# Experts stage: the second product's weight transfers move from SyncE's queue to ScalarE's

## The chip, the cores and the metric

The kernel runs on one core of a Trainium2 chip. The metric is device time in microseconds (us), the median of the timed runs. Engines are named as the profile names them: PE is TensorE, DVE VectorE, ACT ScalarE, POOL GpSimd, SP SyncE. SP computes nothing; its queue issues DMA transfers. ACT and POOL have queues that issue transfers too, between their computing instructions, and every engine works its own queue strictly in order.

## The reference, cut to what matters

Two transformer blocks follow each other. The change touches only the last large piece, the mixture of experts of the second block: every token goes to 2 of 32 experts, and each expert is a gated product.

```python
xs = xf[tok]
hid = jax.nn.silu(lax.ragged_dot(xs, w1, group_sizes)) * lax.ragged_dot(xs, w3, group_sizes)
ys = lax.ragged_dot(hid.astype(xs.dtype), w2, group_sizes) * gate.reshape(-1)[order][:, None].astype(xs.dtype)
```

Here there are 1024 tokens, the model is 1024 wide and an expert 512 wide. w1 and w3 are the weights of the first product ("up"), w2 those of the second ("down").

## The kernel before, in words

The tokens, sorted by expert, are laid out in blocks of 128 slots that each belong to one expert. How many blocks there are is known only at run time (`last_pair`); in the profiled execution it is 36, since 288 up tiles of weights were loaded and a block takes 8. A block b needs 12 weight tiles of 128x1024 float32, 512 KB each: 8 up tiles, which land in `raw_up[:, n]`, and 4 down tiles, which land in `raw_down[:, k]`. Each of these twelve places exists once, so a tile's successor can be asked for only when both halves of the split below have read it.

Float32 products are made of two reduced halves. ACT copies a raw tile into `w_high` (the "raise": `raise_up` L2668, `raise_down` L2678). A second engine subtracts it from the raw tile into `w_low` (the "lower"): DVE for up tiles (`lower_up` L2728), POOL for down tiles (`lower_down` L2591). PE then multiplies high by high, high by low and low by high: `step` L2646 to L2648 for up tiles, `multiply_down` L2631 for down tiles. The split tiles stand in a ring of 6 slots.

The engines run one software pipeline, skewed by a block: step b raises, lowers and multiplies the up tiles of block b, and does the down part of block b-1. Steps 0 and 1 are written out, steps 2 to 35 run in a loop of two steps per turn (`over_pairs`), and a tail finishes block 35. The order is written out by hand in each engine's `step`:

- ACT: raise up 0 and 1; `x_high` L2698; raise up 2 to 5; `hid_high` L2683; raise up 6 and 7; `store` L2688, a DMA that writes the output of block b-2 after waiting for `y_out` from DVE; raise down 0; `silu` L2712; raise down 1 to 3.
- DVE: lower up 0; `hidden` L2734; lower up 1; `x_low` L2759; lower up 2 to 5; `lower_hidden` L2738; `copy_out` L2748; lower up 6 and 7.
- POOL: `gather` (L2580 to L2584, an indirect DMA for block b+2), then lower down 0 to 3.
- PE: up tiles 0 to 7; transposes of the next x; `multiply_down(b-1)`; transposes of the hidden block.
- SP: `load`, 8 up tiles of block b, each after the lower of its predecessor (semaphore `up_low`), and then `load_down(b-1)`, 4 down tiles, each after POOL's lower of its predecessor (semaphore `down_low`).

The expert's number is read from the table `m.owner` into a register by `value_load`, once in `load` and once in `load_down`. The wait that the change carries from one queue to the other is this, k = 0 to 3:

```python
earlier(sp, down_low, 4 * (b - 1) + k + 1)
sp.dma_start(raw_down[:, k], d["w2"][ds(expert, 1), :, k].rearrange("a p n -> p (a n)")
```

With b standing for the block whose tiles are loaded, it says that POOL has lowered tile k of the block before it.

Of the kernel before, what the change touches and what calls it, by code (L numbers as in the profile page):

```python
# [27 lines left out]
ds = bass.ds  # L28
# [26 lines left out]
EXPERTS = GROUPS * PER_GROUP  # L55
# [8 lines left out]
HT = DE // P  # L64
# [566 lines left out]
def two_banks(ps, bank):  # L631
    return ps[:, bank:bank + 2, :].rearrange("p b (k n) -> p (b k) n", n=P)
# [1838 lines left out]
def stage_experts(nc, d, m):  # L2471
# [4 lines left out]
    with ExitStack() as ctx:  # L2476
# [3 lines left out]
        def sem(name):  # L2480
            return nc.alloc_semaphore(name)

        def two(name):
# [4 lines left out]
        raw_up, raw_down = m.raw_up, m.raw_down  # L2488
# [15 lines left out]
        up_loaded, down_loaded = m.up_loaded, m.down_loaded  # L2504
        indexed, gathered, stored = (two("moe_" + n) for n in ("indexed", "gathered", "stored"))
        up_high, up_low, up_used, down_high, down_low, down_used = (sem("moe_" + n) for n in (
            "up_high", "up_low", "up_used", "down_high", "down_low", "down_used"))
# [6 lines left out]
        def up_slot(n):  # L2514
            return n % RING

        def down_slot(k):
            return (UPS + k) % RING

        def over_pairs(eng, body):  # L2520


            last = eng.value_load(m.last_pair[0:1, 0:1], min_val=SLOTS_MIN // (2 * P) - 1,
                                  max_val=BLOCKS // 2 - 1)
            for s in range(2):
                body(0, s, s)
            with eng.Fori(1, last + 1) as i:
                for s in range(2):
                    body(i, s, 2)
            return last  # L2530

        def earlier(eng, sem, value):

            if not isinstance(value, int) or value > 0:
                eng.wait_ge(sem, value)

        def up_slot_free(eng, b, n):

            if n < 2:
                earlier(eng, up_used, 8 * b - 1 + n)  # L2540
            elif n < RING:
                earlier(eng, down_used, 4 * (b - 2) + n - 1)
            else:
                eng.wait_ge(up_used, 8 * b + n - 5)

        @block.sync
        def _(sp):
            def load_down(b):
                if isinstance(b, int) and b == 0:
                    return  # L2550
                expert = sp.value_load(m.owner[0:1, ds(b, 1)], min_val=0, max_val=EXPERTS - 1)
                for k in range(HT):

                    earlier(sp, down_low, 4 * (b - 1) + k + 1)
                    sp.dma_start(raw_down[:, k], d["w2"][ds(expert, 1), :, k].rearrange("a p n -> p (a n)")
                                 ).then_inc(down_loaded[k], 16)

            def load(i, s, before):
                b = 2 * i + s
                if isinstance(b, int) and b == 0:  # L2560
                    return
                expert = sp.value_load(m.owner[0:1, ds(b, 1)], min_val=0, max_val=EXPERTS - 1)
                for n in range(UPS):
                    j, k = n // HT, 2 * (n % HT)

                    earlier(sp, up_low, 8 * (b - 1) + n + 1)
                    sp.dma_start(raw_up[:, n].rearrange("p (k n) -> p k n", k=2),
                                 d["w13"][ds(expert, 1), :, j, k:k + 2].rearrange("a p k n -> p (a k) n")
                                 ).then_inc(up_loaded[n], 16)
                if before:  # L2570
                    load_down(b - 1)

            last = over_pairs(sp, load)
            load_down(2 * last + 1)

        @block.gpsimd
        def _(pool):
# [85 lines left out]
        @block.scalar  # L2663
        def _(act):
            def raise_up(b, n):
                act.wait_ge(up_loaded[n], 16 * (b + 1))
                up_slot_free(act, b, n)
                act.activation(w_high[:, up_slot(n)], raw_up[:, n], ACT.Copy).then_inc(up_high, 1)  # L2668

            def raise_down(b, k, end=False):  # L2670
                act.wait_ge(down_loaded[k], 16 * (b + 1))
                if end:

                    act.wait_ge(down_used, 4 * (b - 1) + k + 1)
                else:

                    act.wait_ge(up_used, 8 * (b + 1) + k + 3)
                act.activation(w_high[:, down_slot(k)], raw_down[:, k], ACT.Copy).then_inc(down_high, 1)  # L2678

            def turned_hidden(b):  # L2680
                act.wait_ge(hid_turned, b + 1)
                earlier(act, down_used, 4 * b)
                act.activation(hid_high[:].rearrange("p k n -> p (k n)"), ps[:, 4, :], ACT.Copy  # L2683
                               ).then_inc(hid_high_out, 1)

            def store(b, o):
                act.wait_ge(y_out, NH * b + NH)
                act.dma_start(d["y_rows"][ds(b * P, P), :], y[o]).then_inc(stored[o], 16)  # L2688

            def step(i, s, before):  # L2690
                b = 2 * i + s
                ahead = 2 if before else RING
                for n in range(ahead):
                    raise_up(b, n)
                act.wait_ge(x_turned, b + 1)

                earlier(act, up_used, 8 * b)
                act.activation(x_high[:], two_banks(ps, 0), ACT.Copy).then_inc(x_high_out, 1)  # L2698
                for n in range(ahead, RING):
                    raise_up(b, n)  # L2700
                if before:
                    turned_hidden(b - 1)
                for n in range(RING, UPS):
                    raise_up(b, n)
                if before > 1:
                    store(b - 2, s)
                if before:
                    raise_down(b - 1, 0)
                act.wait_ge(up_used, 8 * b + 4)

                earlier(act, hid_turned, b - 1)
                act.activation(hid[s], ps[:, 2, :], ACT.Silu).then_inc(silued, 1)  # L2712
                if before:
                    for k in range(1, HT):
                        raise_down(b - 1, k)

            last = over_pairs(act, step)
            turned_hidden(2 * last + 1)
            for k in range(HT):
                raise_down(2 * last + 1, k, end=True)  # L2720
            store(2 * last, 0)
            store(2 * last + 1, 1)

        @block.vector
# [405 lines left out]
```

## Time and profile before

| | us |
|---|---|
| timed runs, median (3 runs) | 3482.81 |
| timed runs, lowest and highest | 3479.39, 3483.36 |
| profiled execution, own time | 3477.42 |
| profiled execution, span of its core | 3475.6 |
| experts stage in it, steps 2 to 35 | some 2726 to 3400 from the span's start |

The trace gives for each engine its instructions with start and duration, the idle time before one and what ended it. Times are from the span's start. A row of the timeline merges instructions of one line that follow each other without a pause (x3, x4); "idle before" stands in brackets. The DMA share is the mean busy share of the core's 16 DMA engines, and PEclk is the granted clock of TensorE, 1.00 for 2.4 GHz and 0.50 for 1.2 GHz. Where an instruction waits for several semaphores, the view names the one that came last.

### The profile page before, as it was taken

The numbers are of one execution on the slowest core, as the hardware profiler recorded it, in microseconds if no ns is written. First come the engines' busy times: TensorE is split into PE (matmuls) and PEld (weight loads), VectorE is DVE, ScalarE is ACT, GpSimd is POOL, SyncE is SP. The second block draws the span as 40 slices with busy tenths as digits, with TensorE's granted clock in tenths as the row PEclk, the third lists the DMA queues.
The fourth block names the chain that finished last, engine by engine and source line by source line (L and its number), as shares of the span: only waits on it lengthen the run. The fifth ranks groups of instructions, "written<-read, shape, count | busy, mean of one in ns | idle before, by whom it ended". The sixth has DMA issues, their size and how long they took to land. (4 is left out here: it accounts for less than half of the span.)

```text
span 3475.6 us, 40486 instructions
## 1 busy us (share of the span) xinstructions
PE 3099.1 (89%) x14608; PEld 2226.9 (64%) x14608; DVE 1532.0 (44%) x2000; ACT 1130.9 (33%) x1517; POOL 1123.1 (32%) x567
## 2 busy tenths in 40 slices
PE   8999999989999999859898997999594899999993
PEld 5666666468888788624444445999342777777772
DVE  4444444421111211346300444444425778778775
ACT  3333332011111122211210221222201677777773
POOL 1101110223333344410001113222000588787784
PEclk9999999999999999979899998999796999999996
DMA  2000002111111132155200014000303899999995
GB/s 92 25 19 19 31 19 81 77 49 48 48 48 48 65 129 95 63 201 181 99 25 29 25 43 164 13 13 1 134 1 133 320 370 372 366 371 371 368 374 212
DMA packets 116290, 446.94 MB, mean 129 GB/s; under 512 B 14658, under 2 KB 15618, under 8 KB 111314
## 3 DMA queue, kind: packets, MB, share of 16 engines
q1 hardware_dynamic: 102740, 393.66, 30.7%
q0 software_dynamic: 7984, 28.66, 2.5%
q10 hardware_dynamic: 5456, 23.10, 1.6%
q8 instruction: 75, 1.23, 0.1%
q14 instruction: 35, 0.29, 0.0%
HBM read 401.18 MB, written 44.10 MB: 128 GB/s over the span
## 5 line engine op out<-in xcount | busy, mean ns | idle before, releaser
L2728 DVE TENSOR_TENSOR moe_w_low<-moe_raw_up,moe_w_high 128x1024 fp32r<-128x1024 f32 x288 | 438.3, 1560 | 153.7 <-ACT moe_w_high L2668 153.7
L2591 POOL TENSOR_TENSOR moe_w_low<-moe_raw_down,moe_w_high 128x1024 fp32r<-128x1024 f32 x144 | 419.6, 2944 | 143.2 <-ACT moe_w_high L2678 143.2
L2668 ACT ACTIVATE moe_w_high<-moe_raw_up 128x1024 fp32r<-128x1024 f32 x288 | 304.7, 1061 | 188.8 <-PE ps L2631 111.6
L91 PE MATMUL ps<-x1T_high,w_up_high 128*128 128x512 f32 x704 | 274.7, 390 | 3.5 <-PEq L2949 3.5
L91 PE MATMUL ps<-x1T_low,w_up_high 128*128 128x512 f32 x704 | 274.4, 390 | 0.0
L91 PE MATMUL ps<-x1T_high,w_up_low 128*128 128x512 f32 x704 | 274.3, 390 | 0.0
L2646 PE MATMUL ps<-moe_w_high,moe_x_high 128*128 128x512 f32 x576 | 228.7, 397 | 4.0 <-DVE moe_x_low L2759 4.0
L2648 PE MATMUL ps<-moe_w_high,moe_x_low 128*128 128x512 f32 x576 | 225.7, 392 | 0.0
L2647 PE MATMUL ps<-moe_w_low,moe_x_high 128*128 128x512 f32 x576 | 225.3, 391 | 0.0
L781 POOL TENSOR_TENSOR w_up_high<-w_up,consts 128x1024 fp32r<-128x1024 f32 x44 | 83.6, 1899 | 382.7 <-PE ps L91 285.3
L446 DVE TENSOR_REDUCE top<-ps 128x1 f32<-128x256 f32 (+7 forms) x128 | 91.0, 753 | 240.3 <-PE ps L342 240.2
L279 POOL TENSOR_TENSOR qkv_low<-qkv_raw,qkv_high 128x1024 fp32r<-128x1024 f32 x22 | 53.6, 2436 | 438.0 <-ACT qkv_high L578 438.0
L296 PE MATMUL ps<-x0T_high,qkv_high 128*128 128x512 f32 x384 | 162.9, 424 | 22.8 <-DVE x0T_low L483 10.0
L80 PE MATMUL ps<-xT,w_cols 128*128 128x512 f32 x384 | 170.7, 598 | 0.0
L80 PE MATMUL ps<-w_rows,xT 128*128 128x512 f32 x384 | 165.5, 593 | 0.0
L561 ACT ACTIVATE probs<-ps,top 128x256 f32<-128x256 f32 (+7 forms) x128 | 94.0, 739 | 216.4 <-DVE top L446 216.4
L2678 ACT ACTIVATE moe_w_high<-moe_raw_down 128x1024 fp32r<-128x1024 f32 x144 | 147.3, 1056 | 33.3 <-DVE xT L2748 18.2
L974 POOL TENSOR_TENSOR w_down_low<-w_down,w_down_high 128x1024 fp32r<-128x1024 f32 x44 | 106.1, 2413 | 157.0 <-ACT w_down_high L957 157.0
L2631 PE MATMUL ps<-moe_w_high,moe_hid_high 128*128 128x512 f32 x288 | 101.7, 434 | 61.2 <-POOL moe_w_low L2591 61.1
L91 PEld LDWEIGHTS ps<-x1T_high,w_up_high 128*128 128x128 f32 x704 | 132.5, 188 | 31.5 <-issue 3.9
L298 PE MATMUL ps<-x0T_high,qkv_low 128*128 128x512 f32 x384 | 151.7, 395 | 0.0
L297 PE MATMUL ps<-x0T_low,qkv_high 128*128 128x512 f32 x384 | 151.1, 394 | 0.0
(436 smaller groups left out, 6157.5 us busy)
## 6 DMA issues: line engine op xcount, KB each, us to landing
moe_raw_up<-in_w SPq DMA_DIRECT2D x288, 512.0 KB, 10.4
moe_raw_down<-in_w SPq DMA_DIRECT2D x144, 512.0 KB, 9.7
w_ada<-in_w_ada SPq DMA_DIRECT2D x48, 512.0 KB, 4.9
w_up<-in_ffn_w_up SPq DMA_DIRECT2D x22, 1024.0 KB, 4.8
w_down<-in_ffn_w_down SPq DMA_DIRECT2D x44, 512.0 KB, 3.5
y_rows<-xT ACTq DMA_DIRECT2D x36, 512.0 KB, 8.3
qkv_raw<-in_attn_w SPq DMA_DIRECT2D x22, 512.0 KB, 3.5
y_rows<-zero_rows SPq DMA_DIRECT2D x1, 8192.0 KB, 30.1
```

What stands on the lines that cost most here:

```text
L80: ins = pe.matmul(out, stationary, moving, start=(n == 0), stop=(n == last))
L91: ins = pe.matmul(out, stationary, moving, start=start and n == 0, stop=stop and n == last)
L296: pe.matmul(ps[:, bank, :], w_high[:, s, k, :], x_high[:, k, cols], start=(k == 0), stop=False)
L297: pe.matmul(ps[:, bank, :], w_high[:, s, k, :], x_low[:, k, cols], start=False, stop=False)
L298: return pe.matmul(ps[:, bank, :], w_low[:, s, k, :], x_high[:, k, cols], start=False, stop=(k == DT - 1))
L2591: pool.tensor_tensor(w_low[:, down_slot(k)], raw_down[:, k], w_high[:, down_slot(k)].bitcast(F32), ALU.subtract).then_inc(down_low, 1)
L2646: pe.matmul(ps[:, 2 + j, :], x_high[:, k, :], high, start=first and a == 0, stop=False)
L2647: pe.matmul(ps[:, 2 + j, :], x_high[:, k, :], low, start=False, stop=False)
L2648: ins = pe.matmul(ps[:, 2 + j, :], x_low[:, k, :], high, start=False, stop=last and a == 1)
L2668: act.activation(w_high[:, up_slot(n)], raw_up[:, n], ACT.Copy).then_inc(up_high, 1)
L2678: act.activation(w_high[:, down_slot(k)], raw_down[:, k], ACT.Copy).then_inc(down_high, 1)
L2728: dve.tensor_tensor(w_low[:, up_slot(n)], raw_up[:, n], w_high[:, up_slot(n)].bitcast(F32), ALU.subtract).then_inc(up_low, 1)
```

## The change

`load_down` leaves SP's queue and is written into ACT's, word for word otherwise, its `value_load` and its four waits for `down_low` included. In ACT's `step` it stands right behind `x_high` and ahead of the raises of up 2 to 5; a copy for the last block stands ahead of the tail. SP's queue keeps the up tiles alone. Nothing is added to or taken from what any engine computes, nor from the transfers.

```diff
@@ sync
-            def load_down(b):
-                if isinstance(b, int) and b == 0:
-                    return
-                expert = sp.value_load(m.owner[0:1, ds(b, 1)], min_val=0, max_val=EXPERTS - 1)
-                for k in range(HT):
-
-                    earlier(sp, down_low, 4 * (b - 1) + k + 1)
-                    sp.dma_start(raw_down[:, k], d["w2"][ds(expert, 1), :, k].rearrange("a p n -> p (a n)")
-                                 ).then_inc(down_loaded[k], 16)
-
...
-                if before:
-                    load_down(b - 1)
-
-            last = over_pairs(sp, load)
-            load_down(2 * last + 1)
+
+            over_pairs(sp, load)
@@ scalar
+            def load_down(b):
+                if isinstance(b, int) and b == 0:
+                    return
+                expert = act.value_load(m.owner[0:1, ds(b, 1)], min_val=0, max_val=EXPERTS - 1)
+                for k in range(HT):
+
+                    earlier(act, down_low, 4 * (b - 1) + k + 1)
+                    act.dma_start(raw_down[:, k], d["w2"][ds(expert, 1), :, k].rearrange("a p n -> p (a n)")
+                                  ).then_inc(down_loaded[k], 16)
+
...
                 act.activation(x_high[:], two_banks(ps, 0), ACT.Copy).then_inc(x_high_out, 1)
+                if before:
+                    load_down(b - 1)
                 for n in range(ahead, RING):
                     raise_up(b, n)
...
             last = over_pairs(act, step)
+            load_down(2 * last + 1)
             turned_hidden(2 * last + 1)
```

SP's queue in the loop before, where a step's last up tile (L2567) is followed by the four down tiles (L2555) and these by the next step's read of `owner` (an ISA or REGISTER_ALU row is a wait or register work):

```order
L2567 DMA moe_raw_up<-in_w 128x1024
L2551 ISA
L2551 TENSOR_LOAD owner
L2551 ISA x2
L2535 ISA
L2555 ISA
L2555 DMA moe_raw_down<-in_w 128x1024
...
L2555 DMA moe_raw_down<-in_w 128x1024
L2562 ISA
L2562 TENSOR_LOAD owner
```

The same place in SP's queue of the change, with the lines' new numbers:

```order
L2557 DMA moe_raw_up<-in_w 128x1024
L2552 ISA
L2552 TENSOR_LOAD owner
L2552 ISA x2
L2535 ISA
```

The four down transfers, their waits and one read of `owner` are gone from between two steps' up transfers.

ACT's queue in the loop before, from `x_high` (L2698) over the raises of up 2 to 5 (L2668) to `hid_high` (L2683):

```order
L2698 ACTIVATE moe_x_high<-ps 128x1024
L2535 REGISTER_ALU
L2668 ACTIVATE moe_w_high<-moe_raw_up 128x1024
L2535 REGISTER_ALU
L2668 ACTIVATE moe_w_high<-moe_raw_up 128x1024
L2535 REGISTER_ALU
L2668 ACTIVATE moe_w_high<-moe_raw_up 128x1024
L2535 REGISTER_ALU
L2668 ACTIVATE moe_w_high<-moe_raw_up 128x1024
L2535 REGISTER_ALU
L2683 ACTIVATE moe_hid_high<-ps 128x512
```

The same place in ACT's queue of the change (`x_high` L2695, raises L2655, `hid_high` L2670):

```order
L2695 ACTIVATE moe_x_high<-ps 128x1024
L2676 ISA
L2676 TENSOR_LOAD owner
L2676 ISA x2
L2535 REGISTER_ALU
L2680 ISA
L2680 DMA moe_raw_down<-in_w 128x1024
...
L2680 DMA moe_raw_down<-in_w 128x1024
L2655 ACTIVATE moe_w_high<-moe_raw_up 128x1024 x4
L2670 ACTIVATE moe_hid_high<-ps 128x512
```

The read of `owner`, four waits for `down_low` and four issues now stand between `x_high` and the raise of up 2.

## Rows read from the trace of the kernel before

**Rows 1.** The page: busy time of each engine over the whole span.

```profile
PE 3099.1 (89%) x14608; PEld 2226.9 (64%) x14608; DVE 1532.0 (44%) x2000; ACT 1130.9 (33%) x1517; POOL 1123.1 (32%) x567
```

**Rows 2.** Stretches: length, busy time of PE to POOL, PEclk, DMA share, GB/s.

```profile
2735.00:3395.00 660.00, 605.68 (x2797) 485.30 (x2796) 518.30 (x436) 477.70 (x499) 521.44 (x233) 1.00 0.99 369
2714.00:2735.00 21.00, 17.99 (x80) 14.17 (x81) 19.62 (x14) 16.11 (x18) 14.27 (x6) 1.00 0.86 296
3408.00:3416.00 8.00, 3.85 (x13) 2.89 (x12) 1.89 (x3) 4.38 (x5) 5.75 (x3) 0.79 0.33 126
```

**Rows 3.** Waits in 2735 to 3395: total us, times, longest.

```profile
DVE moe_w_low L2728 <- ACT moe_w_high L2668: 141.7, 33, 4.3
POOL moe_w_low L2591 <- ACT moe_w_high L2678: 128.4, 33, 4.0
```

**Rows 4.** Timeline of POOL, one step: start, us, line, tile.

```profile
2999.55 11.80 POOL L2591 TENSOR_TENSOR moe_w_low<-moe_raw_down,moe_w_high 128x1024 fp32r<-128x1024 f32 x4 [3.85 <-ACT moe_w_high L2678]
3002.28 2.41 POOL L2591 TENSOR_TENSOR moe_w_low<-moe_raw_down,moe_w_high 128x1024 fp32r<-128x1024 f32 x1
3008.00 3.35 POOL L2591 TENSOR_TENSOR moe_w_low<-moe_raw_down,moe_w_high 128x1024 fp32r<-128x1024 f32 x1
3019.49 11.70 POOL L2591 TENSOR_TENSOR moe_w_low<-moe_raw_down,moe_w_high 128x1024 fp32r<-128x1024 f32 x4 [3.93 <-ACT moe_w_high L2678]
```

**Rows 5.** Timeline of DVE in the same step.

```profile
3004.33 1.43 DVE L2728 TENSOR_TENSOR moe_w_low<-moe_raw_up,moe_w_high 128x1024 fp32r<-128x1024 f32 x1 [4.28 <-ACT moe_w_high L2668]
3006.28 2.83 DVE L2728 TENSOR_TENSOR moe_w_low<-moe_raw_up,moe_w_high 128x1024 fp32r<-128x1024 f32 x1
3010.17 2.25 DVE L2728 TENSOR_TENSOR moe_w_low<-moe_raw_up,moe_w_high 128x1024 fp32r<-128x1024 f32 x1
3012.35 1.21 DVE L2728 TENSOR_TENSOR moe_w_low<-moe_raw_up,moe_w_high 128x1024 fp32r<-128x1024 f32 x1
3014.62 1.21 DVE L2728 TENSOR_TENSOR moe_w_low<-moe_raw_up,moe_w_high 128x1024 fp32r<-128x1024 f32 x1
3015.76 0.68 DVE L2738 TENSOR_TENSOR moe_hid_low<-ps,moe_hid_high 128x512 fp32r<-128x512 f32 x1
3016.36 1.27 DVE L2748 TENSOR_TENSOR xT<-ps,mod 128x512 f32<-128x512 f32 x2
```

**Rows 6.** Timeline of ACT in the same step; ACTq is its queue issuing a DMA.

```profile
3003.24 1.06 ACT L2668 ACTIVATE moe_w_high<-moe_raw_up 128x1024 fp32r<-128x1024 f32 x1 [0.30 <-PE ps L2648]
...
3005.62 1.01 ACT L2698 ACTIVATE moe_x_high<-ps 128x1024 fp32r<-128x1024 f32 x1
...
3013.10 1.06 ACT L2668 ACTIVATE moe_w_high<-moe_raw_up 128x1024 fp32r<-128x1024 f32 x1 [2.25 <-PE ps L2631]
...
3017.80 0.34 ACTq L2688 DMA_DIRECT2D y_rows<-xT  x1
3018.34 1.06 ACT L2678 ACTIVATE moe_w_high<-moe_raw_down 128x1024 fp32r<-128x1024 f32 x1 [0.99 <-DVE xT L2748]
...
3019.79 3.01 ACT L2678 ACTIVATE moe_w_high<-moe_raw_down 128x1024 fp32r<-128x1024 f32 x3
...
3028.09 1.06 ACT L2668 ACTIVATE moe_w_high<-moe_raw_up 128x1024 fp32r<-128x1024 f32 x1 [0.31 <-PE ps L2631]
```

**Rows 7.** Timeline of SP's queue: first issue, us to the end of the last, count.

```profile
3002.49 9.35 SPq L2555 DMA_DIRECT2D moe_raw_down<-in_w  x4
3012.77 7.62 SPq L2567 DMA_DIRECT2D moe_raw_up<-in_w  x8
```

**Rows 8.** One line's instructions: SP's transfer issued at 3014.5 (up 3), then `owner` reads (ns).

```profile
DMA to landing us min/median/max: 10.4/10.4/10.4
...
L2551 SPq TENSOR_LOAD <-owner x4: 332/349/447, 3000.7 to 3060.1; - x4
```

**Rows 9.** Timelines behind the loop, block 35: POOL and ACT.

```profile
3399.27 7.10 POOL L2591 TENSOR_TENSOR moe_w_low<-moe_raw_down,moe_w_high 128x1024 fp32r<-128x1024 f32 x3
...
3408.63 0.60 ACT L2683 ACTIVATE moe_hid_high<-ps 128x512 fp32r<-128x512 f32 x1 [8.69 <-PE ps L2656]
```

## The prediction, written before the changed kernel ran

> **What bounds the kernel now.** I began with the page [rows 1]: PE is busy 89% of the span. That is a mean over many stages, and the change touches one, so the stretch of its loop decides. There (the first of [rows 2]) PE is busy 605.68 of 660 us (92%) at a granted clock of 1.00, and the DMA engines show a share of 0.99 at 369 GB/s. Either could pass for the limit. The waits of the stretch [rows 3] speak against both. The two longest are DVE for ACT and POOL for ACT, once in each of 33 steps, and none of the 9 pairs in that view is an engine that waits for a transfer. I therefore followed one step through the timelines and looked for a closed chain without a pause.
>
> A step lasts 19.84 us: POOL's four lowers end at 2999.55 + 11.80 = 3011.35 and one step later at 3019.49 + 11.70 = 3031.19 [rows 4]. The chain between these two ends is:
>
> - POOL's lower of down 3 ends at 3011.35 (the third of [rows 4]).
> - DVE had begun its lower of up 2 at 3010.17, but took 2.25 us over it instead of 1.21 (the third and fourth of [rows 5]); it is held until POOL is through. The next one begins at 3012.35, which is 1.00 us behind POOL's end.
> - DVE runs on without a pause: lowers of up 3 to 5 in steps of (3014.62 - 3012.35) / 2 = 1.135 us, `lower_hidden` at 3015.76, `copy_out` from 3016.36 to 3017.63 [rows 5].
> - ACT waits for this `copy_out` in `store`, issues it at 3017.80 and begins the raise of down 0 at 3018.34 [rows 6].
> - POOL starts 1.15 us later, at 3019.49, and works for 11.70 us [rows 4].
>
> 8.14 us from POOL's end to its start and 11.70 us of POOL's work are 19.84 us. PE is not in this chain, nor is any transfer: up 3 was issued at 3014.5, took 10.4 us [rows 8] and so landed at 3024.9, and ACT raised it at 3028.09 (the last of [rows 6]). The DMA engines are full, yet they deliver 3.1 us early.
>
> The second thing to read is how POOL and DVE treat each other. A lower of POOL lasts 2.41 us by itself (the second of [rows 4]); the one of down 3 took 3.35. DVE's lower of up 1, begun at 3006.28 under POOL's third tile, ends at 3009.11 (the second of [rows 5]); from there to POOL's end at 3011.35 are 2.24 us, one whole lower. The two take turns. Four lowers of POOL would take some 9.4 us by themselves and take 11.80: a step holds it for about 0.4 us at the first tile (3002.28 - 2999.55 is 2.73) and for 1.0 each at the third and the fourth, behind DVE's lowers of up 0 and up 1.
>
> **The change part by part.**
>
> *SP loses four issues, their waits and one read of `owner`.* Today SP is held behind the down tiles: its four issues stretch over 9.35 us, at the pace of POOL's lowers, and the up tiles follow at 3012.77 [rows 7]. Up 0 could be asked for once DVE has lowered its predecessor, at 3004.33 + 1.43 = 3005.76 (the first of [rows 5]), 7 us earlier. Nothing waits for the landing, so this is worth 0. Its cover is the 3.1 us above, and it only grows.
>
> *ACT gains a wait in the middle of its step.* ACT is through with `x_high` at 3005.62 + 1.01 = 3006.63 (the second of [rows 6]). It then reads `owner` (0.35 us by SP's rows for the same read [rows 8]) and issues down 0 and down 1, whose predecessors POOL has lowered at some 3002.3 and 3004.7. Down 2 waits for POOL's third tile (3008.0), and down 3 for the fourth: 3011.35. From 3006.63 to then are 4.7 us, and in them fall the raises of up 2, 3 and 4 today: up 5 begins at 3013.10 behind an idle time of 2.25 us, so these three are done by 3010.85 (the third of [rows 6]). Queued behind the wait are these three, up 5, `hid_high`, up 6 and 7, the store and all raises of the down tiles. DVE waits for the raises, and POOL for the last. The read of `owner` and the first three issues cost nothing, because they lie within these 4.7 us. Only the fourth issue is on the path.
>
> *The price on the chain.* POOL's end is time 0.
>
> - Issue of down 3: SP's fourth ends at 3002.49 + 9.35 = 3011.84 [rows 7], 0.49 behind POOL's end. I take the same 0.49 for ACT: its own issue of the store takes 0.34 us and starts 0.17 behind DVE's end (3017.63 to 3017.80) [rows 5, 6], which is 0.51.
> - From the issue to the next raise: behind the store's issue it is 3018.34 - 3018.14 = 0.20 us [rows 6], with two register instructions between; none stand there in the new order. So between 0.0 and 0.20; I take 0.14, nearer to the only row.
> - Raise of up 2: 1.06 us, and DVE starts 0.03 behind a raise (3003.24 + 1.06 = 3004.30 on ACT, 3004.33 on DVE) [rows 5, 6].
> - DVE's next lower starts one interval of 1.135 us behind.
>
> Together 0.49 + 0.14 + 1.06 + 0.03 + 1.135 = 2.86 us, where it is 1.00 today. A step becomes 1.85 us longer (bounds 1.72 and 1.91). From there on the chain is the same as today, since ACT's raises follow each other in about 1.0 us (three in 3.01 [rows 6]), faster than DVE's lowers. PE spends 605.68 / 660 x 19.84 = 18.2 us on a step's 12 tiles [rows 2], some 1.5 each; behind POOL's end it has one down tile and two up tiles to do before it needs up 2, 4.5 us, and DVE has lowered that by 2.9.
>
> Does POOL's own time stay at 11.70? It shifts as a whole. Up 0 of the next step is raised behind the raises of down 1 to 3, so it too comes some 1.5 to 1.85 us later, and DVE's lowers of up 0 and up 1 again meet POOL's second and third tiles. The lower of up 2 no longer begins under POOL's fourth tile, but by the turns read above it was DVE that was held there, not POOL. Nothing is given back. The Trainium skill's page "SBUF — State Buffer", section "SBUF: two separate sides", has a rule for this: when a DVE instruction with two SBUF inputs meets a GpSimd instruction, the first one keeps the shared port pair for its whole length and the other fully blocks. By that rule the sum stays at 1.85; if the two merely slowed each other, the fourth tile, 0.94 us over its 2.41, would win back about the half of this that falls beside up 2, 0.45, and the sum would be 1.4 (48 us in all). The rows fit the rule.
>
> *Where it counts.* Steps 2 to 35 have the wait: 34 of them. Behind the loop ACT issues block 35's down tiles before `hid_high`; POOL's end there is 3399.27 + 7.10 = 3406.37, and ACT is idle until 3408.63 [rows 9], so this costs 0.
>
> The sum: 34 x 1.85 = 62.9 us on the profiled execution's own 3477.42, which gives 3540.3. The median of the runs shown is 5.4 us (0.15%) above that execution. Against the median the forecast is 3482.8 + 62.9 = 3545.7.
>
> **The rivals.**
>
> *The turns fall otherwise (about 3527).* DVE's lower of up 0 is ready 0.35 us before POOL's second tile ends (3004.33 against 3004.69) [rows 4, 5]. Moved by a little it would fall under the third tile, up 1 would fall behind the fourth, and POOL would be held once less: 1.1 us won, of which some 0.55 is lost again because `x_low` and up 2 come behind the late up 1. A step then costs 1.3 us more: 44 us. For it: the margin is small. Against it: the new order brings up 0 earlier within POOL's work, not later, as the raise no longer waits for PE but only for ACT itself.
>
> *No change (3483).* ACT is idle for 2.25 us before up 5 anyway [rows 6], and 28% of the stretch [rows 2]; one may hope that the wait falls there. Against it: the four lowers of DVE need the raises one by one, and three of them would start only when today they are all done. Or the move is a matter of queues alone: the Trainium skill's page "DMA: Bandwidth & Descriptors", section "Issuing engines are not separate DMA queues", says that transfers of all engines interleave on the same DMA engines and that spreading them saves only issue time. By that rule alone the result would be 0, and what decides here is the wait beside the issue, which it does not speak of.
>
> *Faster: the DMA engines are the limit after all (about 3427).* With SP free, up tiles are asked for up to 7 us earlier, and a share of 0.99 leaves room for the claim. A step could then shrink to PE's own 18.2 us: 34 x 1.64 = 56 us less. It would decide once a raise waited for a landing; the early 3.1 us and the empty list of waits for DMA [rows 3] speak against it.
>
> *Much slower: PE loses its clock, or ACT's issue is dearer (3580 and more).* PE's pauses grow from 19.84 - 18.2 = 1.6 to about 3.5 us a step. A stretch with PE busy for 17.99 of 21 us stayed at 1.00; one with 3.85 of 8 fell to 0.79 [rows 2]. At 1.2 GHz throughout, the 18.2 us would double and PE would set the step, some 560 us more in all. In the forecast PE is busy 18.2 of 21.7 us, so nearer to the first. An issue that took ACT 1 us more would add 34 us.
>
> **How the numbers follow.** The forecast has 0.80: its own range is 1.72 to 1.91 us by 34, 3541 to 3548, widened by the spread of the runs (4 us) to 3537 to 3552. Other turns, or a POOL that wins something back: 0.09, 3524 to 3531. Much slower: 0.05. No change: 0.03. Faster: 0.03. The range 3526 to 3555 takes the forecast and most of the first rival, and the rest of it stands for a term that is mis-sized by some 0.3 us. A measurement of this kernel tells 0.2% (7 us) from no change. Faster by more has 0.03, within it 0.03, slower 0.94.
>
> **What would show it.** A step of 21.7 us between POOL's fourth lowers; ACT idle for some 5 to 6 us before the raise of up 2, put down to POOL's lower, 34 times (about 190 us); that raise beginning 0.6 us behind POOL's end; DVE's lower of up 2 at 1.2 us instead of 2.25; POOL's four still at 11.7; PE at 84% of the stretch and clock 1.00; DMA at about 338 GB/s (369 x 19.84 / 21.7). It would be wrong if POOL's four took less than 11.3, if a raise waited for a landing, or if the clock fell in the loop.

## The result: 57 us slower, by a wait in ACT's queue and the issue behind it

| | before | changed |
|---|---|---|
| timed runs, median (4 and 4) | 3481.10 us | 3538.53 us |
| lowest and highest | 3476.30, 3483.36 | 3537.54, 3543.77 |
| profiled execution, own time | 3477.42 | 3537.54 |
| one step of the experts' loop | 19.85 | 21.62 |

The ratio is 1.017, with a 95% interval of 1.0152 to 1.0188: 57.4 us by the medians. The change has 34 steps with the new wait, and 34 x (21.62 - 19.85) = 60.2 us, which is the difference between the two profiled executions (60.1 us). So what lies outside this loop adds nothing that can be seen.

The stretch that [rows 2] shows of before, in the changed kernel (length; busy time of PE, PE's loads, DVE, ACT, POOL; PEclk, DMA share, GB/s):

```profile
2735.00:3395.00 660.00, 561.26 (x2573) 444.69 (x2574) 459.92 (x399) 413.35 (x462) 392.53 (x213) 1.00 0.94 341
```

Every engine is idler than before, and so are the DMA engines (341 GB/s for 369). No resource became the limit; a wait did. The waits of the same stretch, which answer to [rows 3]:

```profile
POOL moe_w_low L2578 <- ACT moe_w_high L2665: 260.6, 31, 8.5
DVE moe_w_low L2728 <- ACT moe_w_high L2655: 197.0, 60, 3.8
ACT moe_w_high L2655 <- POOL moe_w_low L2578: 186.2, 30, 6.3
```

The third row is new. L2655 is `raise_up`: ACT now stands still for POOL once in each of 30 steps, 6.2 us at a time (the prediction looked for 5 to 6). POOL and DVE wait for ACT in turn, POOL for 8.4 us a step where it was 3.9.

One step in the timelines, first ACT, to be read beside [rows 6]:

```profile
3005.59 1.99 ACT L2655 ACTIVATE moe_w_high<-moe_raw_up 128x1024 fp32r<-128x1024 f32 x2
3007.23 0.34 ACTq L2680 DMA_DIRECT2D moe_raw_down<-in_w  x1
3007.48 1.01 ACT L2695 ACTIVATE moe_x_high<-ps 128x1024 fp32r<-128x1024 f32 x1
3007.80 6.77 ACTq L2680 DMA_DIRECT2D moe_raw_down<-in_w  x3
3014.67 3.90 ACT L2655 ACTIVATE moe_w_high<-moe_raw_up 128x1024 fp32r<-128x1024 f32 x4 [6.18 <-POOL moe_w_low L2578]
...
3022.37 0.36 ACTq L2685 DMA_DIRECT2D y_rows<-xT  x1
3022.85 1.06 ACT L2665 ACTIVATE moe_w_high<-moe_raw_down 128x1024 fp32r<-128x1024 f32 x1 [1.89 <-DVE xT L2748]
```

The first issue (down 0) is out at 3007.23, before `x_high` has even begun at 3007.48: the engine is still at the raise of up 1, which ends at 3005.59 + 1.99 = 3007.58. So the queue keeps its order, but an issue doesn't wait until the instruction ahead of it has been computed. The next three stretch over 6.77 us at POOL's pace, and the four raises of up 2 to 5 come in a block behind them.

DVE and POOL in the same step, to be read beside [rows 4, 5]:

```profile
3015.77 1.23 DVE L2728 TENSOR_TENSOR moe_w_low<-moe_raw_up,moe_w_high 128x1024 fp32r<-128x1024 f32 x1 [2.78 <-ACT moe_w_high L2655]
3016.91 1.22 DVE L2728 TENSOR_TENSOR moe_w_low<-moe_raw_up,moe_w_high 128x1024 fp32r<-128x1024 f32 x1
...
3020.91 1.28 DVE L2748 TENSOR_TENSOR xT<-ps,mod 128x512 f32<-128x512 f32 x2
```

```profile
3002.44 11.63 POOL L2578 TENSOR_TENSOR moe_w_low<-moe_raw_down,moe_w_high 128x1024 fp32r<-128x1024 f32 x4 [8.46 <-ACT moe_w_high L2665]
3014.03 0.18 POOL L2567 COPY slot_index<-slot_token 128x1 uint32 x1
3014.28 0.19 POOL L2570 TENSOR_TENSOR moe_spare<-consts 128x1 f32<-128x1 f32 x1
...
3023.99 11.70 POOL L2578 TENSOR_TENSOR moe_w_low<-moe_raw_down,moe_w_high 128x1024 fp32r<-128x1024 f32 x4 [8.40 <-ACT moe_w_high L2665]
```

POOL ends at 3002.44 + 11.63 = 3014.07. From there:

| behind POOL's end | before | forecast | changed |
|---|---|---|---|
| ACT raises up 2 | had been done | 0.63 | 0.60 |
| DVE starts the lower of up 2 | held until 0 | 1.72 | 1.70 |
| DVE starts the lower of up 3 | 1.00 | 2.86 | 2.84 |
| ACT raises down 0 | 6.99 | 8.84 | 8.78 |
| POOL starts again | 8.14 | 9.99 | 9.92 |
| POOL's four lowers last | 11.70 | 11.70 | 11.70 |

The row of ACT raising down 0 in the forecast is the old 6.99 plus 1.85.

### The profile page after: what moved, and what is told of

It reads as the page before. It is cut to its first block and busy times, and to the rows that moved or that the text cites. A ratio compares the mean times of both kernels' runs of the same rounds, so it can differ in the third digit from the quotient of the medians.

```text
span 3535.5 us, 40506 instructions
## 1 busy us (share of the span) xinstructions
PE 3101.2 (88%) x14608; PEld 2222.2 (63%) x14608; DVE 1514.9 (43%) x2000; ACT 1100.9 (31%) x1518; POOL 1028.2 (29%) x567
## 3 DMA queue, kind: packets, MB, share of 16 engines
q8 instruction: 74, 1.21, 0.1%
## 5 line engine op out<-in xcount | busy, mean ns | idle before, releaser
L2728 DVE TENSOR_TENSOR moe_w_low<-moe_raw_up,moe_w_high 128x1024 fp32r<-128x1024 f32 x288 | 417.0, 1490 | 231.9 <-ACT moe_w_high L2655 231.9
L2655 ACT ACTIVATE moe_w_high<-moe_raw_up 128x1024 fp32r<-128x1024 f32 x288 | 284.6, 1048 | 244.1 <-POOL moe_w_low L2578 204.8
```

What stands on the lines that cost most here:

```text
L2728: dve.tensor_tensor(w_low[:, up_slot(n)], raw_up[:, n], w_high[:, up_slot(n)].bitcast(F32), ALU.subtract).then_inc(up_low, 1)
```

## The experiments

Three theories stood against each other. A: the wait in front of the raises is the cost, and what it costs is set by where DVE and POOL take turns. B: ACT as the issuer is the cost (a read of `owner` and four issues a step). C: the transfers themselves suffer (two queues, late landings, full DMA engines). Medians and ratios are against before in the same series (3480.9 to 3481.6 us).

| kernel | median us | ratio, 95% interval | step us |
|---|---|---|---|
| the change | 3538.53 | 1.0170 (1.0152 to 1.0188) | 21.62 |
| interleaved | 3479.87 | 0.9998 (0.9988 to 1.0008) | 19.85 |
| wait_only | 3523.92 | 1.0128 (1.0111 to 1.0145) | 21.15 |
| raises_ahead1 | 3504.25 | 1.0069 (1.0052 to 1.0086) | 20.52 |
| raises_ahead2 | 3491.36 | 1.0033 (1.0022 to 1.0043) | 17.9 to 23.8 |
| ahead2_quarter | 3481.23 | 0.9996 (0.9986 to 1.0005) | 19.84 |
| quarter_down | 3480.57 | 1.0000 (0.9990 to 1.0009) | 19.85 |
| last_late | 3482.45 | 0.9998 (0.9988 to 1.0008) | 19.85, two pairs 18.9 and 22.1 |
| store_later | 3506.19 | 1.0077 (1.0060 to 1.0093) | 20.6 |
| inter_store_later | 3505.27 | 1.0051 (1.0027 to 1.0074) | 20.6 |
| dve_down | 3407.54 | 0.9786 (0.9769 to 0.9802) | 17.74 |
| dve_down_after | 3406.93 | 0.9784 (0.9768 to 0.9801) | 17.8 |

The length of a step is the time between the ends of two last lowers of a down tile in the profiled execution.

**interleaved: the issues without the wait.**

```diff
                 act.activation(x_high[:], two_banks(ps, 0), ACT.Copy).then_inc(x_high_out, 1)
-                if before:
-                    load_down(b - 1)
+                expert = down_expert(b - 1) if before else None
                 for n in range(ahead, RING):
                     raise_up(b, n)
+                    if before:
+                        load_down_tile(expert, b - 1, n - 2)
```

`down_expert` is the `value_load` of `load_down`, `load_down_tile` its wait and issue for one k.

> The change with its four issues spread: down k is issued on ACT behind the raise of up k+2, so down 3 stands behind the raise of up 5, which waits for PE's last down tile anyway. Theory A (the wait in front of the raises is the cost; an issue runs in the queue while the ACT engine still computes the raise ahead of it): each wait is already satisfied when it is reached, the step stays at 19.8 us, 0 to +7 us against before (3481 to 3488). Theory B (ACT as the issuer is the cost: one read of owner, 0.3 us, and four issues at some 0.57 us each in its queue, 2.6 us a step): at least +40 us. Theory C (two queues with deep transfers beside each other slow the landings): also slower, and raises waiting for DMA.

Measured: 3479.87, no difference from before. ACT's timeline shows where the issues went:

```profile
3009.97 1.06 ACT L2655 ACTIVATE moe_w_high<-moe_raw_up 128x1024 fp32r<-128x1024 f32 x1 [0.30 <-PE ps L2618]
3010.11 0.34 ACTq L2682 DMA_DIRECT2D moe_raw_down<-in_w  x1
3011.53 1.06 ACT L2655 ACTIVATE moe_w_high<-moe_raw_up 128x1024 fp32r<-128x1024 f32 x1 [0.49 <-PE ps L2618]
3011.66 0.34 ACTq L2682 DMA_DIRECT2D moe_raw_down<-in_w  x1
```

Each issue lies inside the raise ahead of it: the queue issues while the engine computes. The same transfers, from the same queue, with the same four waits cost nothing once every wait is satisfied when it is reached. C falls for this kernel, and so does B as the cause of the whole; what an issue does cost behind an unsatisfied wait is read from the next run.

**wait_only: the wait without the issues.**

```diff
                 act.activation(x_high[:], two_banks(ps, 0), ACT.Copy).then_inc(x_high_out, 1)
+                if before > 1:
+                    act.wait_ge(down_low, 4 * (b - 1))
                 for n in range(ahead, RING):
```

> The kernel before with one wait more and nothing moved: in steps 2 to 35 ACT waits behind x_high for POOL's four lowers (the semaphore down_low at 4(b-1)); SP keeps all transfers. Theory A: the raise of up 2 begins some 0.1 us behind POOL's end instead of the 0.60 of the change, DVE's next lower at 2.35 instead of 1.00: 34 x 1.3 = +45 us against before, 3526. Theory B (issues) and C (two queues): 0, since no transfer has moved.

Measured: 3523.92, which is 42.6 us more, where A said 45 and the others 0. POOL, ACT and DVE in one step:

```profile
3000.97 6.65 POOL L2591 TENSOR_TENSOR moe_w_low<-moe_raw_down,moe_w_high 128x1024 fp32r<-128x1024 f32 x2
```

```profile
3007.74 3.90 ACT L2668 ACTIVATE moe_w_high<-moe_raw_up 128x1024 fp32r<-128x1024 f32 x4 [5.73 <-POOL moe_w_low L2591]
```

```profile
3008.83 1.23 DVE L2730 TENSOR_TENSOR moe_w_low<-moe_raw_up,moe_w_high 128x1024 fp32r<-128x1024 f32 x1 [2.29 <-ACT moe_w_high L2668]
```

The raise begins 0.12 us behind POOL's end (3007.62). So of the 1.77 us a step that the change costs, 1.30 are the wait with the late raise (21.15 for 19.85) and 0.47 the one issue that stands between them. By the medians the change is 14.6 us slower than wait_only.

**raises_ahead1 and raises_ahead2: how late may the wait stand?** `load_down` is moved behind the raise of up 2 (the diff), or behind those of up 2 and 3 (with 2 for both 1s).

```diff
-                if before:
-                    load_down(b - 1)
-                for n in range(ahead, RING):
+                for n in range(ahead, ahead + 1 if before else RING):
                     raise_up(b, n)
+                if before:
+                    load_down(b - 1)
+                    for n in range(ahead + 1, RING):
+                        raise_up(b, n)
```

> The change with load_down one raise later: x_high, raise of up 2, load_down with its four waits, raises of up 3 to 5. Theory A with turns (DVE's lower of up 2 is held until POOL's end and runs to 1.0 us behind it): the raise of up 3 ends at 0.60 + 1.06 = 1.66 behind POOL's end and is needed at 1.00, so 0.7 us a step, 34 x 0.7 = +24 us (3505). Without turns (DVE lowers up 2 before POOL's end): up 3 is needed at once and the cost stays near 1.8 - 1.1 = 0.7 to 1.8 us. Theory B: as the change, +57.

Measured: 3504.25, 23 us more, with every step at 20.5 us; 24 had been expected from DVE being held on up 2 until POOL's end. DVE's rows show both halves of it, the held lower of up 2 and then the pause for up 3. The cost by itself doesn't tell turns from no turns, since the range expected without turns began at the same 0.7 us:

```profile
3004.30 2.25 DVE L2730 TENSOR_TENSOR moe_w_low<-moe_raw_up,moe_w_high 128x1024 fp32r<-128x1024 f32 x1
3007.15 3.50 DVE L2730 TENSOR_TENSOR moe_w_low<-moe_raw_up,moe_w_high 128x1024 fp32r<-128x1024 f32 x3 [0.61 <-ACT moe_w_high L2655]
```

> The change with load_down two raises later: x_high, raises of up 2 and 3, load_down with its four waits, raises of up 4 and 5. Theory A with turns: DVE is busy with up 2 and up 3 until 2.14 us behind POOL's end, and the raise of up 4 ends at 1.66: 0 us a step, within 7 us of before, although ACT still waits for POOL some 2 us in each step. Theory B: as the change, +57.

Measured: 3491.36, 10 us more where 0 was expected. Fifteen of the steps are 19.85 us; nearly all others come in pairs, 18.9 and then 22.1, twice 17.9 and then 23.8. Three steps of POOL, then ACT in the middle one:

```profile
2966.01 11.77 POOL L2578 TENSOR_TENSOR moe_w_low<-moe_raw_down,moe_w_high 128x1024 fp32r<-128x1024 f32 x4 [3.87 <-ACT moe_w_high L2665]
...
2985.94 10.71 POOL L2578 TENSOR_TENSOR moe_w_low<-moe_raw_down,moe_w_high 128x1024 fp32r<-128x1024 f32 x4 [3.94 <-ACT moe_w_high L2665]
...
3007.00 11.71 POOL L2578 TENSOR_TENSOR moe_w_low<-moe_raw_down,moe_w_high 128x1024 fp32r<-128x1024 f32 x4 [7.82 <-ACT moe_w_high L2665]
```

```profile
2989.33 1.06 ACT L2665 ACTIVATE moe_w_high<-moe_raw_down 128x1024 fp32r<-128x1024 f32 x1 [1.09 <-DMA moe_raw_down<-in_w]
```

ACT, which now asks for the four down tiles within 2.86 us (SP before: 9.35), waits for the last of them, which takes 11.3 us to land. The raise of up 0 is late by this, DVE's lower of it falls under POOL's third tile instead of the second, and POOL is held once less: 10.71 us instead of 11.77. This is the rival of the prediction in which the turns fall otherwise. The next step gives more than that back, as POOL now starts only 3007.00 - 2996.65 = 10.35 us behind its end.

**ahead2_quarter.** Is it the landing that starts this? The same kernel with smaller down transfers:

```diff
-                    act.dma_start(raw_down[:, k], d["w2"][ds(expert, 1), :, k].rearrange("a p n -> p (a n)")
+                    act.dma_start(raw_down[:, k, 0:D // 4],
+                                  d["w2"][ds(expert, 1), :, k, 0:D // 4].rearrange("a p n -> p (a n)")
```

> raises_ahead2 (load_down on ACT behind the raises of up 2 and 3) with down transfers of 256 columns instead of 1024, so the second product is computed from partly other weights. raises_ahead2 cost 10 us where 0 was expected, with steps of 18.9, 19.8 and 22.1 us in turn; in its trace the raise of down 3 once waits 1.1 us for its landing, up 0 follows late and DVE and POOL then meet at other tiles. If this late landing starts the unequal steps: all steps 19.85 us and within 7 us of before. If the 2 us wait for POOL itself costs: again about +10 us.

Measured: 3481.23, no difference from before, and all steps at 19.84. It was the landing. The wait for POOL behind two raises costs nothing by itself.

**quarter_down: are the DMA engines a limit before?** The same cut in SP's `load_down` of the kernel before.

> The kernel before, but each down transfer of the loop brings only the first 256 of 1024 columns (the rest of a raw down tile keeps what it held, so the experts' second product is computed from other weights); every instruction, wait and semaphore stays. 1.5 MB less of 7.3 MB a step. Chain theory (no landing is on the chain): within 7 us of before (3481), DMA share down from 0.99 to about 0.8, landings in 4 to 7 us instead of 10.4. Rival (the DMA engines limit the loop and early requests could have made it faster): up to 34 x 1.6 = 55 us faster.

Measured: 3480.57, no difference. The up tiles' landings fell less than expected, to a median of 8.9 us where 4 to 7 had been written. The stretch of [rows 2]:

```profile
2735.00:3395.00 660.00, 603.91 (x2788) 483.47 (x2788) 518.82 (x435) 475.60 (x499) 519.74 (x234) 1.00 0.81 289
```

A share of 0.99 had not been a limit: 80 GB/s less are moved, and the step stays as it is.

**last_late: one wait fewer.** The issues of down 0 to 2 stay where the change has them, that of down 3 goes behind the raise of up 5.

```diff
-                if before:
-                    load_down(b - 1)
+                expert = down_expert(b - 1) if before else None
+                if before:
+                    for k in range(HT - 1):
+                        load_down_tile(expert, b - 1, k)
                 for n in range(ahead, RING):
                     raise_up(b, n)
+                if before:
+                    load_down_tile(expert, b - 1, HT - 1)
```

> The change with the issue of down 3 alone moved behind the raise of up 5; down 0 to 2 stay ahead of the raises. ACT then waits for POOL's third tile only, 3.35 us before POOL's end, so the raise of up 2 begins 1.7 us later than before and up 3 and 4 follow at 1 us each: the last of them ends about where it is needed. Theory A with turns (DVE is held on up 2 until POOL's end): 0, within 7 us of before (3481). Without turns: 34 x 1.7 = +58 us, as the change.

Measured: 3482.45, no difference (the profiled execution has two pairs of steps of 18.9 and 22.1 us, all others 19.85). ACT still waits, for POOL's third tile, and the raises of up 2 to 4 are late, but DVE's rows have the lengths of those of before. ACT's queue and engine, then DVE:

```profile
3010.79 2.18 ACTq L2682 DMA_DIRECT2D moe_raw_down<-in_w  x3
3013.07 2.95 ACT L2655 ACTIVATE moe_w_high<-moe_raw_up 128x1024 fp32r<-128x1024 f32 x3 [1.97 <-PE ps L2618]
```

```profile
3013.48 1.21 DVE L2770 TENSOR_TENSOR moe_x_low<-ps,moe_x_high 128x1024 fp32r<-128x1024 f32 x1
3014.61 5.66 DVE L2739 TENSOR_TENSOR moe_w_low<-moe_raw_up,moe_w_high 128x1024 fp32r<-128x1024 f32 x4
```

The trace puts this idle time down to PE; by the order of the queue it is the issue of down 2, and so POOL's third tile, that ACT waited for.

The raise of up 2 ends at 3013.07 + 1.06 = 3014.13, and DVE is at `x_low` until it turns to up 2 at 3014.61. Up 3 and 4 are raised by some 3015.1 and 3016.0; a DVE that nobody held would want them at 3015.75 and 3016.9. So the late raises are in time with or without turns, and the +58 us expected without turns doesn't follow. The run shows that three of the four waits cost nothing where they stand; it doesn't tell the two readings apart.

**store_later and inter_store_later: shortening the chain.** The store's wait for `copy_out` stands in the chain ahead of the raise of down 0. Both kernels exchange the two, one on the kernel before and one on interleaved:

```diff
-                if before > 1:
-                    store(b - 2, s)
                 if before:
                     raise_down(b - 1, 0)
+                if before > 1:
+                    store(b - 2, s)
```

> The kernel before with two lines of ACT's step exchanged: the raise of down 0 goes ahead of the store, whose wait for DVE's copy_out stands in the chain. The raise is then held by PE's third up tile, about 0.8 us earlier: a step of 19.0 us, 34 x 0.8 = 27 us faster (3454), if the DMA engines (share 0.99) and the turns of DVE and POOL follow. If the landings become late instead (down 3 has the least time), only a part of it or nothing, with raises waiting for DMA.

Measured: 3506.19, which is 25 us slower where 27 us faster was expected. No raise waits for a landing. DVE and POOL:

```profile
3009.06 9.82 DVE L2728 TENSOR_TENSOR moe_w_low<-moe_raw_up,moe_w_high 128x1024 fp32r<-128x1024 f32 x3
```

```profile
3008.75 2.40 POOL L2591 TENSOR_TENSOR moe_w_low<-moe_raw_down,moe_w_high 128x1024 fp32r<-128x1024 f32 x1 [5.63 <-ACT moe_w_high L2678]
3011.51 9.64 POOL L2591 TENSOR_TENSOR moe_w_low<-moe_raw_down,moe_w_high 128x1024 fp32r<-128x1024 f32 x3 [0.36 <-ACT moe_w_high L2678]
```

POOL's first tile did come earlier, as meant. But it now starts 0.31 us ahead of DVE's lower of up 6 instead of behind it, and DVE is held for it and for the tiles that follow: three lowers (up 6, up 7 and the next up 0) take 9.82 us, where three in a row took 3.50 in raises_ahead1. PE then waits for DVE's lowers, twice a step:

```profile
PEld ps L2646 <- DVE moe_w_low L2728: 101.1, 64, 2.1
```

> interleaved (down transfers issued by ACT, down k behind the raise of up k+2) with the same exchange of store and raise of down 0. If SP's freed queue is worth anything once the chain is shorter (up tiles asked for earlier, landings 8.5 instead of 10.4 us), this is faster than store_later; if not, the two are alike at about 3454.

Measured: 3505.27, with runs from 3478.68 to 3508.41; three of ten lie at 3479 to 3483 and the others at 3502 to 3508. The profiled execution took 3506.86 and has the steps of store_later. There is no trace of one of the faster three, so whether they had other turns stays open. At the median the freed SP queue shows no gain; whether the three owe theirs to it is open too.

**dve_down and dve_down_after: without the turns.** POOL's four lowers go to DVE, behind its lowers of up 6 and 7. One kernel starts from before, the other from the changed kernel with its wait in front of the raises.

```diff
@@ gpsimd
                 gather(b + 2, s, i + 2)
-                if before:
-                    lower_down(b - 1)
...
-            lower_down(2 * last + 1)
@@ vector
+            def lower_down(b):
+                for k in range(HT):
+                    dve.wait_ge(down_high, 4 * b + k + 1)
+                    dve.tensor_tensor(w_low[:, down_slot(k)], raw_down[:, k],
+                                      w_high[:, down_slot(k)].bitcast(F32), ALU.subtract
+                                      ).then_inc(down_low, 1)
...
                 for n in range(RING, UPS):
                     lower_up(b, n)
+                if before:
+                    lower_down(b - 1)
...
             copy_out(2 * last, 0, last)
+            lower_down(2 * last + 1)
             copy_out(2 * last + 1, 1, last)
```

> The kernel before, with the four lowers of the down tiles on DVE (behind up 6 and 7, 1.14 us each) instead of POOL (2.35 us each); POOL only gathers. If the turns of DVE and POOL are what sets the step (8 x 1.1 + 4 x 2.35 = 18.2 us of taking turns in 19.84), the step falls to what PE needs, 18.2 to 18.5 us: 34 x 1.35 to 1.6 = 46 to 55 us faster, 3426 to 3435. The DMA engines would then have to bring 7.3 MB in 18.3 us, 401 GB/s: if they can't, a part of the gain is lost and raises wait for landings. If the turns did not matter, DVE's 17.3 us of work in one queue would give nothing or make it slower.

Measured: 3407.54, which is 74 us faster than before and 131 faster than the change. DVE's lowers of the four down tiles, and the loop:

```profile
3004.85 4.70 DVE L2724 TENSOR_TENSOR moe_w_low<-moe_raw_down,moe_w_high 128x1024 fp32r<-128x1024 f32 x4
```

```profile
2735.00:3330.00 595.00, 595.00 (x2821) 494.45 (x2820) 586.78 (x572) 485.11 (x502) 71.11 (x99) 1.00 1.02 409
```

Four lowers in 4.70 us instead of 11.70. PE is busy all the time, and the step is 17.74 us: PE bounds the loop now, and ACT waits for it at most of its raises, 331 times in three rows of which this is the largest. DVE is close behind, busy for 586.78 of 595 us.

```profile
ACT moe_w_high L2658 <- PE ps L2638: 42.0, 134, 0.4
```

The move takes away two things at once, the turns (some 2.3 us a step) and the longer time that POOL takes over a lower by itself (2.35 us for DVE's 1.14). How the 2.1 us a step divide between them isn't shown.

> The changed kernel, with the same move of the four lowers to DVE. DVE is through with down 3 some 2 us before ACT comes to load_down, so the four waits are satisfied when they are reached. Theory A (only the wait costs): as dve_down, within 7 us, and no longer 57 us slower than its counterpart. Theory B (the issues on ACT cost): slower than dve_down by up to 34 x 2.6 us less what is hidden. If the DMA engines limit dve_down, the freed SP queue may show as a gain here.

Measured: 3406.93, as dve_down. The changed queues, which cost 57 us beside POOL's lowers, cost nothing beside DVE's, because the four waits are satisfied when ACT comes to them. Here raises do wait for landings, at 408 GB/s:

```profile
ACT moe_w_high L2645 <- DMA moe_raw_up<-in_w: 43.2, 26, 2.8
ACT moe_w_high L2655 <- DMA moe_raw_down<-in_w: 24.5, 27, 1.5
```

The mean step is as in dve_down, and PE stays busy for 594.73 of 595 us. The waits end before PE runs out of split tiles:

```profile
2735.00:3330.00 595.00, 594.73 (x2818) 493.94 (x2817) 576.59 (x569) 457.96 (x500) 100.50 (x99) 1.00 1.02 408
```

## Why the prediction was right

- **The bound before** [rows 3 to 6]: a chain over POOL, DVE and ACT that no transfer is part of. quarter_down shows the second half, dve_down the first: with the same transfers and the same products the loop lost 2.1 us a step. The cover of 3.1 us, though, was read from up 3 alone. Down 3 is asked for at 3011.50 and raised at some 3021.7, so it has 10.2 us to land; the trace has no landing for it. raises_ahead2, where it took 11.3, shows that the cover was thinner than written.
- **SP's gain of 0.** Up tiles are asked for earlier in the change, and the landings take 5.7 us instead of 10.4 (medians); nothing came of it. interleaved bears this out: it has SP's free queue and landings of 8.5 us, but not the wait, and gained nothing.
- **What is hidden and what is not.** The read of `owner` and three issues lie in front of POOL's end, the fourth is on the path. wait_only and the change differ by 0.47 us a step, near the 0.49 + 0.14 less the 0.12 that a bare wait takes to release the raise.
- **The price on the chain**, 1.85 us a step with bounds 1.72 and 1.91: measured 1.77. The forecast 3546 is 7 us above the 3538.5 measured. Of this, 34 x 0.08 = 2.7 us is the term: the raise came at 0.60 for 0.63 and the chain from DVE's lower of up 3 to POOL's start took 7.08 us for 7.14. The rest is the spread of the runs: the medians differ by 57.4 us and the profiled executions by 60.1, and the median of before fell by 1.7 us with a fourth run.
- **Turns, not slowing.** The choice between 1.85 and 1.4 us a step went to the first: DVE no longer lowers up 2 beside POOL's fourth tile, and POOL's four lowers last 11.63 and 11.70 all the same. The rule of the Trainium skill's page "SBUF — State Buffer", section "SBUF: two separate sides", says that the first one blocks the other fully, and the trace agrees with it in these 11.63 and 11.70 us. raises_ahead1 (23 us, 24 expected) fits as well, but neither it nor last_late can tell the two apart. Not every DVE instruction is held. `x_low`, which has one operand in PSUM (the bank of PE's results), runs its 1.21 us under POOL's fourth tile in the kernel before:

```profile
3009.04 1.21 DVE L2759 TENSOR_TENSOR moe_x_low<-ps,moe_x_high 128x1024 fp32r<-128x1024 f32 x1
```

- **The rivals.** No change and faster were 0.03 each. The page "DMA: Bandwidth & Descriptors" of the Trainium skill, section "Issuing engines are not separate DMA queues", was right about the transfers: spreading them brought nothing, and its result of 0 is that of interleaved. What cost was the wait that moved along with them.
- **The turns that fall otherwise** (0.09) did not come in the change, but in raises_ahead2, twice in last_late and, in another form, in store_later. The prediction priced them as a small gain over the forecast. In raises_ahead2 they won 1.0 us in a step and lost 2.2 in the next, so there the sign was the other; what they would do in the change isn't shown.
- **What the expectations missed.** 0 for raises_ahead2 (a landing that the loop of before had covered), -27 us for store_later and inter_store_later (turns), landings of 4 to 7 us for quarter_down, +58 us for last_late without turns, and -46 to -55 us for dve_down. The last took PE's 18.2 us a step for a floor. PE's busy time in before came out higher than what it needs without pauses, 17.74 us a step.

## What to carry to other kernels

A transfer that is moved to a computing engine's queue takes its wait along: an issue whose wait is satisfied hides behind the engine's own work, an unsatisfied wait doesn't, nor does the issue behind it (1.30 and 0.47 us a step here). Before such a move, find when the awaited instruction ends and put the issue behind the first instruction that can't start earlier anyway (here the raise of up 5), or spread the issues so that each wait is satisfied when it is reached.

A DMA share near 1 doesn't say that the transfers set the time: cut their bytes and look. And where DVE and POOL both work on SBUF operands, look for the turns: add up the times of these instructions by themselves, as if the two were one engine. Here that is some 18.2 of 19.85 us a step, while each engine showed itself busy for less than 80% of the loop. The sum is a warning and not yet the bound; the bound was the chain in which these turns stood.

## What had not been expected of the hardware

- **Time to land follows how the issues are bunched, more than the traffic.** The medians of the up tiles are 10.4 us in the kernel before (369 GB/s in the loop) and 5.7 in the change (341). But interleaved has 8.5 at the same 369 GB/s, wait_only 9.2 at 346 and quarter_down 8.9 at 289, so the traffic alone doesn't give it. In the loop of before SP issues eight up tiles within 7.62 us. In one such burst up 0 lands in 5.7 us, up 3 in 10.4 and up 5 in 11.9. In the change SP issues each as DVE frees its place, and those of the step shown that have a landing take 4.9 to 6.2 us. No run changed the bunching by itself. The changed kernel's medians:

```profile
moe_raw_up<-in_w SPq DMA_DIRECT2D x288, 512.0 KB, 5.7
moe_raw_down<-in_w ACTq DMA_DIRECT2D x140, 512.0 KB, 5.1
```

- **The most that was moved** in a loop was 409 GB/s (dve_down).
- **POOL's smallest instructions pay for the turns too.** The copy of a 128x1 index takes 0.18 us in the change, where DVE is idle beside it. Before, where DVE lowers beside it, 1.18; the 128x1 addition behind it takes 0.19 and 1.06. The timeline of POOL in the kernel before:

```profile
3011.29 1.18 POOL L2580 COPY slot_index<-slot_token 128x1 uint32 x1
3012.55 1.06 POOL L2583 TENSOR_TENSOR moe_spare<-consts 128x1 f32<-128x1 f32 x1
```

- **Who starts first matters.** In store_later a POOL instruction starts 0.31 us ahead of a DVE instruction instead of behind it, and an expected gain of 27 us became a loss of 25. That this one order did it is read from the rows; no run shifted it alone.
